# Two fp32 sums over partitions taken from an upper and a lower part instead, on one core of a Trainium2 chip

## What is computed

```python
xn = rmsnorm(x, norm1_g)                        # first norm
z = xn @ w_in + b_in                            # one projection for four mixers
# mixer C: a causal depthwise convolution of width 31, then
o_c = silu(layernorm(conv(h_ext, conv_w, conv_b), conv_ln_g, conv_ln_b))
merged = sum over i of sigmoid(xn @ w_gate_i + b_gate_i) * (o_i @ w_branch_i)
x = x + merged @ w_out
g, up = split(rmsnorm(x, norm2_g) @ w_gate_up, 2)   # second norm
x = x + (silu(g) * up) @ w_down

def rmsnorm(x, g):
    return x * rsqrt(mean(x * x) + eps) * g     # the mean is over the features of a token

def layernorm(x, g, b):
    xc = x - mean(x)
    return xc * rsqrt(mean(xc * xc) + eps) * g + b
```

## Time and profile before

| | |
|---|---|
| Time, median of 3 runs | 1083.68 us (1083.01 to 1084.06) |
| The profiled execution: its time, and the span of its core | 1083.58 us, 1081.8 us |
| TensorE busy | 1076.5 us, 8587 matmuls |
| VectorE, ScalarE, GpSimd busy | 706.8, 591.7, 451.9 us |

### The profile page before, as it was taken

How to read it: one execution, slowest core, us unless ns; L and a number is a source line. 1 busy time by engine, 2 the same in 40 slices (tenths; PEclk the granted TensorE clock), 3 DMA queues, 4 the chain that set the end, 5 groups by cost and what they waited for, 6 DMA issues and landing times.

```text
span 1081.8 us, 20569 instructions
## 1 busy us (share of the span) xinstructions
PE 1076.5 (100%) x8587; PEld 1055.2 (98%) x8587; DVE 706.8 (65%) x1019; ACT 591.7 (55%) x900; POOL 451.9 (42%) x251
## 2 busy tenths in 40 slices
PE   9999999999999999999999999999999999999999
PEld 8999989999999999999999998999999999999998
DVE  7698689565775555555549856795567765555543
ACT  6555674777455444444446456657765464444431
POOL 2777655673732111101177866657737221111000
PEclk9999999999999999999999999999999999999999
DMA  8755444444556766555554544434554655555552
GB/s 262 283 176 168 143 146 128 128 148 155 175 170 197 204 205 191 169 164 171 178 149 157 169 161 152 149 119 144 150 157 153 224 166 173 158 167 163 180 172 83
DMA packets 62492, 181.46 MB, mean 168 GB/s; under 512 B 16544, under 2 KB 19232, under 8 KB 61728
## 3 DMA queue, kind: packets, MB, share of 16 engines
q1 hardware_dynamic: 61392, 176.07, 52.3%
q10 hardware_dynamic: 1008, 4.08, 1.0%
HBM read 174.90 MB, written 7.27 MB: 168 GB/s over the span
## 4 chain that ended last, share of the span: by engine, by line
PE 98%; DMA 1%; ACT 0%; POOL 0%; DVE 0%; SPq 0%; issue 0%; POOLq 0%
PE ps L443 31%; PE ps L448 30%; PE ps L444 30%; DMA x<-in_x 1%; PE ps L463 0%; PE ps L648 0%; PE ps L541 0%; PE ps L765 0%; PE ps L591 0%; PE ps L458 0%; PE ps L670 0%; PE ps L599 0%; PE ps L736 0%; PE ps L486 0%; PE ps L563 0%; PE ps L519 0%
## 5 line engine op out<-in xcount | busy, mean ns | idle before, releaser
L443 PE MATMUL ps<-x_hi,w_hi 128*128 128x288 f32 x1952 | 583.0, 299 | 1.1 <-POOL x_lo L1776 0.5
L444 PE MATMUL ps<-x_lo,w_hi 128*128 128x288 f32 x1952 | 575.8, 295 | 0.0
L448 PE MATMUL ps<-x_hi,w_lo 128*128 128x288 f32 x1952 | 574.0, 294 | 0.0
L923 ACT ACTIVATE w_hi<-raw 128x1024 fp32r<-128x1024 f32 x314 | 325.8, 1051 | 144.3 <-PE ps L448 126.7
L1781 POOL TENSOR_TENSOR w_lo<-raw,w_hi 128x1024 fp32r<-128x1024 f32 x129 | 331.7, 2583 | 160.7 <-ACT w_hi L923 160.3
L443 PEld LDWEIGHTS ps<-x_hi,w_hi 128*128 128x128 f32 x1952 | 365.7, 187 | 7.7 <-issue 4.5
L448 PEld LDWEIGHTS ps<-x_hi,w_lo 128*128 128x128 f32 x1952 | 367.5, 188 | 0.0
L444 PEld LDWEIGHTS ps<-x_lo,w_hi 128*128 128x128 f32 x1952 | 366.5, 188 | 0.3
L1289 DVE TENSOR_TENSOR w_lo<-raw,w_hi 128x1024 fp32r<-128x1024 f32 x185 | 232.5, 1258 | 118.8 <-ACT w_hi L923 118.8
L1805 POOL TENSOR_TENSOR work<-work,rs 128x288 f32<-128x288 f32 x44 | 35.7, 810 | 237.5 <-ACT work L1250 237.5
L448 PE MATMUL ps<-h_hi,w_lo 128*128 128x288 f32 x352 | 104.4, 296 | 0.0
(11 more groups left out here) (262 smaller groups left out, 1055.2 us busy)
## 6 DMA issues: line engine op xcount, KB each, us to landing
raw<-in_w_up SPq DMA_DIRECT2D x88, 512.0 KB, 4.1
raw<-in_w_z SPq DMA_DIRECT2D x66, 512.0 KB, 3.6
raw<-in_w_gate SPq DMA_DIRECT2D x64, 512.0 KB, 3.6
raw<-in_w_branch SPq DMA_DIRECT2D x32, 512.0 KB, 3.6
raw<-in_w_down SPq DMA_DIRECT2D x32, 512.0 KB, 3.7
raw<-in_w_out SPq DMA_DIRECT2D x16, 512.0 KB, 3.6
raw<-in_w_down SPq DMA_DIRECT2D x16, 384.0 KB, 3.2
kv<-in_state ACTq DMA_DIRECT2D x2, 1024.0 KB, 5.2
```

The lines of the kernel that those rows point to most:

```text
L443: pe.matmul(out, wh, rh, start=start, stop=False)
L444: pe.matmul(out, wh, rl, start=False, stop=False)
L448: return pe.matmul(out, w_lo[:, slot, u * UNIT:(u + 1) * UNIT], rh, start=False, stop=stop)
L923: act.activation(w_hi[:, slot, :], raw[:, slot, :], ACT.Copy).then_inc(hi_done, 1)
```

## The change

The second norm's sum and the sum for the convolution's variance are taken by `sum_of_parts`. For the variance VectorE makes the two parts behind its reduction, as it does for the gMLP's norm. For the second norm GpSimd makes them behind its last addition of squares, and TensorE waits for a new event, `n2_parts`, that both instructions raise.

```diff
@@ mixers, on TensorE
                 yield from at("cv_var")
                 pe.wait_ge(E("cv_sq_added"), l1)
-                sum_of(5, added, "cv_var")
+                sum_of_parts(5, "cv_var")
@@ behind the second block of the feed-forward, on TensorE
-                        pe.wait_ge(squares, (2 * l + 1) * (KC - 1))
-                        sum_of(7, sq[:, 0, :], "n2_sums")
+                        pe.wait_ge(E("n2_parts"), 2 * l1)
+                        sum_of_parts(7, "n2_sums")
@@ add_chunks, on VectorE
-                if event.startswith("cv"):
+                if event == "cv_added":
                     ins.then_inc(E(event), 1)
                 else:
                     link(ins, 0)
                     parts_of(added, event)
@@ add_squares, on GpSimd
+                if n % 2 == 0:
+                    pool.wait_ge(squares, (n + 1) * (KC - 1))
+                    pool.tensor_copy(part_hi, sq[:, 0, :]).then_inc(E("n2_parts"), 1)
+                    pool.wait_ge(E("n2_parts"), n + 1)
+                    pool.tensor_tensor(part_lo, sq[:, 0, :], part_hi.bitcast(f32), ALU.subtract).then_inc(E("n2_parts"), 1)
```

## The result

The changed kernel takes 1085.17 us (median of 21 runs, 1084.73 to 1085.98) against 1083.58 us before (21 runs): 1.59 us or 0.16% more, ratio 1.0016 with a 95% interval of 1.001 to 1.0022. The forecast was +1.34 us.

A forecast was written before the change was run, and what follows sets the result against it. PE, with 98% of the chain that ended last, was taken to bound the kernel. 2 x 0.87 lost less 2 x 0.20 gained made +1.34 us, 1085.0 us on the median, with a range from 1082.8 to 1086.8.

The forecast's parts named there:

- The matmuls: On PE, four fp32 sums replaced by sums by parts: 0.20 us gained each where PE doesn't wait, 0.80 in all.
- The Trainium skill's four passes: On PE, four passes for a true FP32 matmul; set aside because the trace has the sum at 0.48 us.
- the estimate beside the page: On PE, two passes given back per sum, 2 x 0.135 = 0.27 us, 1.1 us for the four.
- Convolution's variance: VectorE's added cast and subtraction stand behind GpSimd's weight instructions, PE's sum is late: 0.87 us lost in each layer.
- the two engines take turns when both queue: At the variance, VectorE's cast goes between GpSimd's two weight instructions, its subtraction behind the second, ending at 208.77.
- Second norm: GpSimd's added cast and subtraction end at 338.5 to 338.6, before PE's sum at 339.05: hidden, 0.20 gained each layer.
- the cast first: At the second norm, GpSimd's cast begins 0.01 to 0.02 us ahead of VectorE's first weight instruction and goes first.
- the sign: At the second norm, VectorE's weight instruction beside GpSimd's cast takes 1.5 us or more instead of 1.21.
- The first: Rival: at the second norm VectorE goes ahead of GpSimd's cast, PE waits; +2.8 us, 1086.5, in both layers; chance 0.26.
- The second: Rival: no wait at the variance or the second norm; -0.80 us, 1082.9; chance 0.13.
- third: Rival: variance's cast waits for both GpSimd weight instructions, second norm also late; +3.3 us, 1087.0; chance 0.05.

The follow-up runs named there:

- e8: Kernel before, with the second norm's fp32 sum made eight more times in each layer; 1091.53 us in its one run, 7.9 more than before.
- e1: Changed kernel with GpSimd's parts and the second norm's sum taken back to fp32, leaving the change at the variance alone; 1085.34 us, ratio 1.0015.
- e3: Changed kernel with VectorE's reduction for the variance written to PSUM, where the cast and subtraction read it; 1082.97 us, ratio 0.9994.
- e7: Changed kernel with the variance's sum and the steps that wait for it one gate block later in the order; 1082.82 us, ratio 0.9992.
- e2: Changed kernel with the variance's sum taken back to fp32, leaving the change at the second norm alone; 1083.37 us, ratio 0.9997.
- e4: Changed kernel with an empty instruction and its hop ahead of GpSimd's cast for the second norm; 1085.65 us, 1.97 over the kernel before.
- e10: Kernel with the variance's reduction in PSUM, plus an empty instruction and hop ahead of GpSimd's second-norm cast; 1083.94 us, 0.32 over the kernel before.
- e6: Against e3, GpSimd's two parts counted on the semaphore of the squares instead of one of their own; 1082.99 us.
- e9: Kernel before, with GpSimd's cast and subtraction for the second norm added and their result unused; 1083.65 us, interval 0.9993 to 1.0011.

## Why the prediction was right

**The matmuls: 0.20 us a sum.** Measured 0.20 where PE doesn't wait (0.61 to 0.41, layer 1's second norm), and e8 puts the fp32 sum at 0.485. The Trainium skill's four passes (FP8 and Floating Point Precision, TensorE Precision Notes) were set aside as too many, and that reading was mistaken: a quarter of e8's 0.485 us is 0.121 us, which at the upper clock level of 2.4 GHz (the clock granted in e8 is 1.0) makes 291 clocks for 288 columns, so by this estimate four passes fit. What doesn't fit is taking the 0.135 us of ordinary matmuls for a pass, as the estimate beside the page did.

**Convolution's variance: 0.87 us lost in each layer.** Measured 0.88 and 0.87. Each step came as worked out: cast 2.19 (forecast 2.20), subtraction 2.50 (2.50), PE 0.06 behind it, the first matmul at 0.40. The step that carried it is that the two engines take turns when both queue: the cast went in between GpSimd's two weight instructions, and the second went ahead of the subtraction. First come, first served would give the same order in each of these rows, as it does in the earlier trace rows; no run tells the two rules apart, and the forecast needs only what they share. e1 shows that this place has all of the loss, e3 that it goes when the pair has no business with GpSimd, e7 that it goes when PE comes later.

**Second norm: the cast first, the parts hidden.** The order was right, by 0.03 us in both layers, and e2 gives -0.31 against -0.40. That a working to 0.01 or 0.02 us, from a hop seen once, came out on the right side is partly luck: the hop ahead of the cast was 0.06 us (336.67 + 0.81 = 337.48 to 337.54) and not 0.08. The delay of VectorE's first weight instruction was sized a little high: it took 1.47 us, 0.26 more than 1.21, where 0.3 to 0.45 more was worked out and 1.5 or more was named as the sign. The end of the subtraction was taken to be some 0.5 us ahead of PE; it was 0.7 in layer 1 and 0.05 in layer 0, since the margin moves with a transfer that the prediction took as fixed, and that the parts were still in time in layer 0 is luck too. This accounts for 0.09 of the 0.25 us by which +1.59 exceeds +1.34; the rest isn't traced and is no larger than the scatter between runs. The prediction took 2.2 us as what can be told from no change; with 21 runs of each kernel the interval, 1.1 to 2.4 us more, lies clear of it.

**The rivals.** The first has the right mechanism, since turning the order moves the parts by 1.1 us, to 3.26 us behind VectorE's start where 339.61 - 336.28 = 3.33 was worked out, but its price was taken from one margin of 2.77 us: for both layers 1.44 us more than the forecast was worked out, where e4 and e10 measure 0.4 and 1.0. The second and third, no wait at all and a cast that waits for both of GpSimd's instructions, didn't occur; the cast's 2.19 us shows that it waited for one.

## What to carry to other kernels

An instruction's undisturbed duration says little about when its result is ready if the other of VectorE and GpSimd is busy all the time with long operations on SBUF: count one whole operation of the other engine for each dependent step, and look at which step is queued when the other's next one is. Two short steps behind 2.4 us operations cost 4.7 us here instead of 0.8, and the slack of 3.7 us was gone. Two small edits took the wait away: letting both steps read their common operand from PSUM (e3), or letting the consumer come one block later (e7).

## What was not expected of the hardware

An order decided by 0.01 to 0.04 us between two engines is the same in both layers of all six profiles that have the parts without the hop (the changed kernel, e2, e3, e6, e7, e9). That it is so steady because both starts follow ScalarE instructions that stand one behind the other (L1157 and L923) is argued, not shown. One empty instruction and its hop, which put the cast 0.07 or 0.08 us behind, turn it in both layers of e4 and e10. The margin of PE to the same two engines moves by about 1 us between profiles, with the landing of a transfer.
